# Two attention stages: value products of two heads issued together, projections cut in blocks, rotations moved

## What is computed

```
idx = einsum('bthd,bsd->bths', qi, k_idx)
score = einsum('bth,bths->bts', wi, relu(idx))       # top-k over s picks the keys of the A heads
oa = einsum('bhtk,bkr->bthr', pa, c_sel)             # latent values, then o_a = oa @ w_uv per head
lb = einsum('bthd,bshd->bhts', qb, k_b) + cum_f[t] - cum_f[s]   # causal
ob = einsum('bhts,bshd->bthd', softmax(lb), v_b)
```

```
q, k, v, xq = split(u @ w_in);  q, k = rope(q), rope(k)
p = exp(s - m) / (sum(exp(s - m)) + exp(sink - m));  o = p @ v
```

## Time and profile before

| what | value |
|---|---|
| median of 3 runs | 1451.8 us (1450.42 to 1453.05) |
| profiled execution, its own time | 1447.94 us |
| span of its trace | 1446.6 us, so 1.3 us lie around it |
| PE busy | 1400.8 us, 97% of the span |
| DVE, ACT, POOL busy | 65%, 50%, 16% |
| mean granted PE clock | 0.988 |

### The profile page before, as it was taken

One profiled execution on the slowest core, in us unless ns is written; L12 is line 12 of the kernel. 1 busy time (PEld: TensorE's weight loads), 2 busy tenths in 40 slices (PEclk: granted clock), 3 DMA queues, 4 the chain that ended last, 5 costly groups with the idle time before them and its releaser, 6 DMA issues.

```text
span 1446.6 us, 23175 instructions
## 1 busy us (share of the span) xinstructions
PE 1400.8 (97%) x9623; PEld 1256.9 (87%) x9623; DVE 940.2 (65%) x1510; ACT 723.5 (50%) x1055; POOL 224.3 (16%) x186
## 2 busy tenths in 40 slices
PE   7999999999999999999899999999999999899998
PEld 6887799999898899997777899999689888799997
DVE  4854477667786866667467276566556888666555
ACT  4534355545453555453555464445356775554443
POOL 4561300000000000000722500000123333100000
PEclk9999999999999999999999999999999999899999
DMA  7522145654563456552422355555344435355551
GB/s 279 205 101 117 59 178 201 223 197 178 177 230 140 175 180 227 176 190 102 174 88 88 117 203 176 215 192 177 137 182 147 147 117 205 117 186 200 194 192 58
DMA packets 36698, 240.40 MB, mean 166 GB/s; under 512 B 3889, under 2 KB 6257, under 8 KB 9202
## 3 DMA queue, kind: packets, MB, share of 16 engines
q1 hardware_dynamic: 36594, 238.92, 45.3%
HBM read 236.27 MB, written 2.64 MB: 165 GB/s over the span
## 4 chain that ended last, share of the span: by engine, by line
PE 80%; DVE 9%; ACT 4%; issue 3%; POOL 3%; DMA 2%; SPq 0%; ACTq 0%; DVEq 0%
PE ps L398 22%; PE ps L361 15%; PE ps L362 15%; PE ps L363 15%; POOL wlo L298 2%; ACT whi L290 1%; PE ps L528 1%; DVE ar L2155 1%; PE ps L533 1%; PE ps L855 1%; PE ps L1663 1%; DMA raw<-in_up 1%; DVE wlo L312 1%; PE ps L509 1%; PE ps L1026 1%
## 5 line engine op out<-in xcount | busy, mean ns | idle before, releaser
L361 PE MATMUL ps<-XS,whi 128*128 128x256 f32 x2088 | 599.7, 287 | 4.6 <-DVE wlo L307 2.9
L362 PE MATMUL ps<-XS,whi 128*128 128x256 f32 x2088 | 594.8, 285 | 0.0
L363 PE MATMUL ps<-XS,wlo 128*128 128x256 f32 x2088 | 594.6, 285 | 0.0
L312 DVE TENSOR_TENSOR wlo<-raw,whi 128x2048 fp32r<-128x2048 f32 x163 | 372.4, 2287 | 127.1 <-ACT whi L290 127.1
L290 ACT ACTIVATE whi<-raw 128x2048 fp32r<-128x2048 f32 x203 | 386.9, 1906 | 132.7 <-PE ps L398 81.9
L361 PEld LDWEIGHTS ps<-XS,whi 128*128 128x128 f32 x2088 | 404.8, 194 | 10.8 <-issue 4.5
L362 PEld LDWEIGHTS ps<-XS,whi 128*128 128x128 f32 x2088 | 404.7, 194 | 2.1 <-issue 0.5
L363 PEld LDWEIGHTS ps<-XS,wlo 128*128 128x128 f32 x2088 | 404.5, 194 | 0.0
L398 PE MATMUL ps<-whi,MS 128*128 128x512 f32 x1024 | 290.7, 391 | 0.0
L298 POOL TENSOR_TENSOR wlo<-raw,whi 128x512 fp32r<-128x512 f32 x158 | 207.5, 1346 | 300.2 <-ACT whi L290 216.7
L398 PEld LDWEIGHTS ps<-whi,MS 128*128 128x128 f32 x1024 | 189.8, 188 | 37.5 <-issue 0.4
(11 more groups left out here) (287 smaller groups left out, 1348.7 us busy)
## 6 DMA issues: line engine op xcount, KB each, us to landing
raw<-in_up SPq DMA_DIRECT2D x88, 1024.0 KB, 4.8
raw<-in_down SPq DMA_DIRECT2D x44, 1024.0 KB, 4.8
raw<-in_hg_t SPq DMA_DIRECT2D x16, 1024.0 KB, 4.8
raw<-in_od_t SPq DMA_DIRECT2D x8, 1024.0 KB, 5.4
raw<-in_ev_a SPq DMA_DIRECT2D x6, 1024.0 KB, 9.8
raw<-in_wa_o SPq DMA_DIRECT2D x6, 1024.0 KB, 4.8
raw<-in_hg_o SPq DMA_DIRECT2D x6, 1024.0 KB, 4.9
raw<-in_ev_o SPq DMA_DIRECT2D x4, 1024.0 KB, 6.9
```

What stands on the lines that cost most here:

```text
L312: ve.tensor_tensor(lo[:, 0:w], r[:, 0:w], hi[:, 0:w].bitcast(F32), ALU.subtract).then_inc(w_lo_v)
L361: pe.matmul(d, hi[:, c], S[:, k, 0:256], start=(k == 0), stop=False)
L362: pe.matmul(d, hi[:, c], S[:, k, 256:512], start=False, stop=False)
L363: last = pe.matmul(d, lo[:, c], S[:, k, 0:256], start=False, stop=(k == 7))
```

## The change

`project` can now issue one block at a time. In the even mixer the index scores are issued for two heads in turn (rows 0 to 63, rows 64 to 127), the value products of B heads 2p and 2p+1 together in the odd step, and `post_a` of two heads together in the even step. In the window mixer the value products are issued in pairs as well. Rotation 0 comes behind the projection of the values instead of ahead of it, rotation 1 between the two blocks of `wq+1`, rotations 2 to 4 in steps 1, 3 and 7 instead of 0, 4 and 8. The tiles `wq+2` to `wx+1` go by blocks in steps 0, 1, 5, 6, 8, 9, 11 and 12, where whole tiles stood in steps 3, 7, 10 and 12. ACT's high parts and the DVE's ropes and splits are moved accordingly. The core of the diff:

```diff
-        def project(m, o, ready=None, S=None):
-
-            S = XS if S is None else S
+        def project(m, o, ready=None, blocks=(0, 1)):
+
+            S = XS
-            for i in range(SCHED[m][2] // 1024):
+            for i in blocks[:SCHED[m][2] // 1024]:
...
+            if blocks[-1] == 1:
+                last.then_inc(w_done)
...
-            for h in range(8):
+            for h in range(0, 8, 2):
+
                 pe.wait_ge(e_ac.sem, 3 + h // 4)
                 if h >= 4:
-                    pe.wait_ge(e_re.sem, h - 3)
+                    pe.wait_ge(e_re.sem, h - 2)
                 else:
                     pe.wait_ge(m_ev.sem, 8)
-                q = slice(64 * (h % 2), 64 * (h % 2) + 64)
                 for tt in range(2):
                     a, b = esegs[tt]
                     c = 256 * (h // 2) + 128 * tt
-                    ins = pe.matmul(bank[h % 4][:, a:b], QI[q, c:c + 128], KI[q, 0:b - a], start=True, stop=True)
-                ins.then_inc(e_ix.up())
+                    for r in range(2):
+                        q = slice(64 * r, 64 * r + 64)
+                        ins = pe.matmul(bank[(h + r) % 4][:, a:b], QI[q, c:c + 128], KI[q, 0:b - a], start=True, stop=True)
+                        if tt == 1:
+                            ins.then_inc(e_ix.up())
...
-                if 0 <= i - 4 < 16:
+                if 0 <= i - 4 < 8 and i % 2:
+                    turned_pe(i - 5, 0)
                     turned_pe(i - 4, 0)
-                    value_b(i - 4) if i - 4 < 8 else value_a(i - 12)
-                if 0 <= i - 13 < 8:
-                    post_a(i - 13)
+                    values_b(i - 5)
+                if 8 <= i - 4 < 16:
+                    turned_pe(i - 4, 0)
+                    value_a(i - 12)
+                if 0 <= i - 13 < 8 and i % 2 == 0:
+                    posts_a(i - 14)
...
+        def values_b(h):
+
+            pair_free(h // 2)
             pe.wait_ge(e_ac.sem, AT_VB)
             o = ePAIR[h // 2 % 2]
-            q = slice(64 * (h % 2), 64 * (h % 2) + 64)
-            v = slice(64 * h, 64 * h + 64)
-            pt = ePT[h % 2]
-            pe.matmul(o[q, 0:256], VB[:, v], pt[:, 0:256], start=True, stop=False)
-            pe.matmul(o[q, 128:256], VB[:, 512 + 64 * h:576 + 64 * h], pt[:, 256:384], start=False,
-                      stop=True).then_inc(a_va.up())
+            for r in range(2):
+                pe.matmul(o[64 * r:64 * r + 64, 0:256], VB[:, 64 * (h + r):64 * (h + r) + 64], ePT[r][:, 0:256], start=True, stop=False)
+            for r in range(2):
+                pe.matmul(o[64 * r:64 * r + 64, 128:256], VB[:, 512 + 64 * (h + r):576 + 64 * (h + r)], ePT[r][:, 256:384],
+                          start=False, stop=True).then_inc(a_va.up())
...
+            for r in range(2):
+                pe.wait_ge(e_oa.sem, h + r + 1)
+                pe.matmul(ePAIR[p % 2][64 * r:64 * r + 64, 0:256], WV[:, 64 * (h + r):64 * (h + r) + 64], OA[r], start=True,
+                          stop=True).then_inc(e_po.up())
...
         def window_pe():
             project(wk, bank[4], xs_both(3))
+            accumulate([wv], XS, list(range(8)), 256, [[bank[0]], [bank[1]]], no_wait, True, True)
             filled(3)
             rotate_pe(0, bank[7])
-            accumulate([wv], XS, list(range(8)), 256, [[bank[0]], [bank[1]]], no_wait, True, True)
             project(wq, bank[6])
+            project(wq + 1, bank[5], blocks=(0,))
             pe.wait_ge(r_out.sem, 1)
             rotate_pe(1, bank[7])
+            project(wq + 1, bank[5], blocks=(1,))
...
-                if 0 <= i - 4 < 20:
+                if 0 <= i - 4 < 16 and i % 2:
+                    turned_pe(i - 5, WB)
                     turned_pe(i - 4, WB)
-                    window_value(i - 4) if i - 4 < 16 else cross_value(X0, i - 20, i - 4)
-                for j in range(1, 4):
-                    if i + 2 == 4 * j - 3:
-                        pe.wait_ge(r_in.sem, j + 1)
-                        project(wq + j, bank[6])
-                    if i + 2 == 4 * j - 2:
-                        pe.wait_ge(r_out.sem, j + 1)
-                        rotate_pe(j + 1, bank[7])
-                if i + 2 == 12:
+                    window_values(i - 5)
+                if 16 <= i - 4 < 20:
+                    turned_pe(i - 4, WB)
+                    cross_value(X0, i - 20, i - 4)
+
+                if i in (0, 1):
+                    pe.wait_ge(r_in.sem, 2)
+                    project(wq + 2, bank[6], blocks=(i,))
+                if i in (5, 6):
+                    pe.wait_ge(r_in.sem, 4)
+                    project(wq + 3, bank[6], blocks=(i - 5,))
+                if i in (8, 9):
                     pe.wait_ge(r_in.sem, 5)
-                    project(wx, bank[6])
-                if i + 2 == 14:
+                    project(wx, bank[6], blocks=(i - 8,))
+                if i in (11, 12):
                     pe.wait_ge(r_out.sem, 5)
-                    project(wx + 1, bank[7])
+                    project(wx + 1, bank[7], blocks=(i - 11,))
+                if i in (1, 3, 7):
+                    j = {1: 2, 3: 3, 7: 4}[i]
+                    pe.wait_ge(r_out.sem, j)
+                    rotate_pe(j, bank[7])
...
+        def window_values(i):
+
+            c = i // 2
             o = wV[c % 2]
-            q = slice(64 * r, 64 * r + 64)
-            if r == 0 and c >= 2:
+            if c >= 2:
                 pe.wait_ge(ms_lo.sem, W0 + c - 1)
+            elif c == 1:
+
+                pe.wait_ge(r_in.sem, 3)
             for s in range(2):
-                last = pe.matmul(o[q, 0:256], VN[:, 256 * s + 64 * kvh:256 * s + 64 * kvh + 64],
-                                 wPT[i % 2][:, 256 * s:256 * s + 256], start=(s == 0), stop=(s == 1))
-            last.then_inc(a_va.up())
+                for r in range(2):
+                    kvh = 2 * (c // 4) + r
+                    last = pe.matmul(o[64 * r:64 * r + 64, 0:256], VN[:, 256 * s + 64 * kvh:256 * s + 64 * kvh + 64],
+                                     wPT[r][:, 256 * s:256 * s + 256], start=(s == 0), stop=(s == 1))
+                    if s == 1:
+                        last.then_inc(a_va.up())
...
+            ac.activation(wQ[i % 2], bank[[4, 6, 5, 6, 6][i]][:, :], ACT.Copy, scale=0.125 if i else 1.0).then_inc(r_in.up())
...
             split_act(0)
+            act_weights(wq + 3)
             split_act(1)
+            rope_in_act(2)
+            act_weights(wx)
             for i in range(-2, 26):
-                if i + 2 in (4, 8, 12):
-                    split_act((i + 2) // 4 + 1)
+                if i in (3, 5, 9):
+                    split_act({3: 2, 5: 3, 9: 4}[i])
                 if 0 <= i - 3 < 20:
...
-                for j in range(1, 4):
-                    if i + 2 == 4 * j - 3:
-                        act_weights(wq + j + 2)
-                    if i + 2 == 4 * j - 2:
-                        rope_in_act(j + 1)
-                if i + 2 in (12, 14):
-                    act_weights(wx + (i - 10) // 2 + 2)
-                if i + 2 in (13, 15):
-                    cross_query_act(X0, (i - 11) // 2)
+                if i == 2:
+                    rope_in_act(3)
+                    act_weights(wx + 1)
+                if i == 7:
+                    rope_in_act(4)
+                    act_weights(wo)
+                if i in (10, 13):
+                    j = (i - 10) // 3
+                    cross_query_act(X0, j)
+                    act_weights(wo + 1 + j)
...
-                for j in range(1, 4):
-                    if i + 2 == 4 * j - 1:
-                        rope_dve(j + 1)
-                    if i + 2 == 4 * j:
-                        split_dve(j + 1)
+                if i in (1, 3, 7):
+                    rope_dve({1: 2, 3: 3, 7: 4}[i])
+                if i in (3, 5, 9):
+                    split_dve({3: 2, 5: 3, 9: 4}[i])
```

More of the change, by code:

```diff
@@ L1080, in value_a, with posts_a @@
             pe.matmul(bank[6][:, 128:256], CN[:, 128:256], pt[:, 256:384], start=False, stop=True).then_inc(a_va.up())
-        def post_a(h):
+        def posts_a(h):
             p = 4 + h // 2
-            if h % 2 == 0:
-                pair_free(p)
+            pair_free(p)
             if h == 0:
                 pe.wait_ge(d_wv, 16)
-            pe.wait_ge(e_oa.sem, h + 1)
-            q = slice(64 * (h % 2), 64 * (h % 2) + 64)
-            pe.matmul(ePAIR[p % 2][q, 0:256], WV[:, 64 * h:64 * h + 64], OA[h % 2], start=True, stop=True).then_inc(e_po.up())
+            for r in range(2):
+                pe.wait_ge(e_oa.sem, h + r + 1)
+                pe.matmul(ePAIR[p % 2][64 * r:64 * r + 64, 0:256], WV[:, 64 * (h + r):64 * (h + r) + 64], OA[r], start=True,
+                          stop=True).then_inc(e_po.up())
         def even_act():
```

10 lines of the change are left out of this document (1 added, 9 removed).

## The result

The changed kernel takes 1462.0 us (median of 4 runs, 1459.9 to 1463.4) where before takes 1451.1: 0.75% slower, interval 0.54 to 0.95%. A second comparison (e15) gave 0.46%, interval 0.28 to 0.64%. The prediction was 1449.3 (1444.5 to 1455.5), a gain of 2.5 us. The even mixer did about what was foreseen, and the window mixer lost 12.9 us where the sum had 1.5.

What follows compares the result with a forecast made beforehand. PE was taken to bound the even head loop, with DVE needing nearly as much per window head. Even mixer -4.0 and window mixer +1.5 gave -2.5 us, from 1451.8 to 1449.3, range 1444.5 to 1455.5.

Steps and rivals of the forecast that it cites:

- Column halves: Paired products on PE: matmuls on two column halves run side by side, so a pair costs one member.
- Even mixer, -4.0: Even head loop: value pairs -3.2, posts -1.2, later stall +0.4, sum -4.0 us, bounds 0 and -5.5.
- the posts: Even mixer, heads 0 to 2, in steps that also score: three posts become one pair, 1.16 us less.
- the stall behind it: Even mixer from step 16: the next head's value product waits for DVE's copy behind the post pair, +0.4 us net.
- Window mixer, +1.5: Whole window mixer: reordering -1.5 us plus lower clock +3.0 makes +1.5, bounds -1.5 and +5.
- the DVE chain behind it is as long as before: Window start, rotation 1 to head 0's score: unchanged at 8.1 us, less 0.7 if POOL disturbs less.
- The term for the lower level: Window mixer: lower clock expected twice, 1.7 to 3.4 us each, less the earlier 1.7, so +3.0 us.
- its 1.7: Window mixer: time the kernel before already lost to 6.9 us at the lower clock, subtracted from the new clock cost.
- Window pairs: Window value products in pairs: each saves 1.0 us in steps 5 to 12, the last four only about 0.4 together.
- There PE is the bound: Window steps 5 to 12, with six blocks: PE sets the pace, so each pair saves 1.0 us.
- The tail: Last window heads, no projection left: DVE needs 2.3 us a head; ACT's high parts only trimmed -1.6 to -1.1.
- The slower one: Rival, 21%: window wait for rope 2's split, more lower clock and DVE slowed by POOL; total +1 to +4, about 1454.5.

Runs made afterwards that it cites:

- e15: The changed kernel, unchanged, profiled and compared with before a second time: 1460.5 us, ratio 1.0046.
- e14: The kernel before, unchanged, profiled a second time: 1451.5 us, ratio 0.9995.
- e1: The kernel before with the changed even mixer alone, window mixer as it was: 1444.4 us, ratio 0.9955.
- e4: The changed kernel with ACT's high part of wq+3 behind the split of rope 1 instead of ahead: 1456.1 us, ratio 1.0036.
- e9: The changed kernel with ACT's high part of wx+1 in step 4, behind the exponentials, instead of step 2: 1456.9 us, ratio 1.0028.
- e3: The changed kernel with rotation 0 back ahead of the projection of the values: 1460.7 us, ratio 1.0066.
- e6: The changed kernel with the moves of e3 and e4, and DVE's split of rope 2 ahead of rope 3: 1453.9 us, ratio 1.0007.
- e7: The changed kernel with the low parts of wq, wq+1 and wq+2 written by DVE instead of POOL: 1459.8 us, ratio 1.005.
- e5: The changed kernel with each head's window value product by itself again, unpaired: 1461.1 us, ratio 1.0061.
- e10: The changed kernel with ACT's high parts of steps 10 and 13 behind the exponentials instead of ahead: 1460.2 us, ratio 1.006.
- e11: The changed kernel with the moves of e6, e9 and e10 together: 1451.2 us, ratio 0.9994.
- e13: e11 with rotation 1 ahead of both blocks of wq+1 instead of between them: 1446.5 us, ratio 0.9963.
- e2: e1 plus window value products in pairs at odd steps, nothing else of the window mixer moved: 1446.9 us, ratio 0.9963.
- e12: e1 with a value pair's four matmuls issued head by head instead of alternating column halves: 1446.6 us, ratio 0.9964.

## Why the prediction was right or wrong

**Column halves: right.** A pair of B heads holds PE from 113.52 to 114.32, 0.80 us, where one head held it 0.79.

```profile
113.52 0.65 PE L1051 MATMUL ps<-ar 128*64 128x256 f32 x4
114.00 0.39 PE L1053 MATMUL ps<-ar 128*64 128x128 f32 x4
114.32 0.49 PE L1034 MATMUL ps<-ar 64*128 64x128 f32 x2
```

The rule of the Trainium skill weighed there ("TensorE: Matmul & The Clock Gate", part 3, "The mechanism") would have given 1.6. The rule is on weight loads alone, and that a pair then costs two members was the prediction's reading of it. The trace does not bear it out for column halves.

**Even mixer, -4.0: right in sum, in part by luck.** With equal lower clock (3.4 us each) the head loop is 64.1 us against 66.7 in e14, and with 6.8 us each 65.6 (e15) against 68.3: -2.6 and -2.7. So the loop itself gave 1.3 us less than the 4.0 foreseen. Up to the last score 3.4 us are saved, 3.1 of them value pairs, so the posts gave 0.3 of their 1.2: only two of them stood there, not three. And the stall behind it was sized too small: from the last score on the loop takes 9.8 us instead of 9.0, where the term had +0.4. In exchange PE's wait inside the norm behind it fell from 1.7 to 0.6 us, which no step had; its cause was not looked into. That makes -3.7. The measured -0.45% of e1 (-0.26 to -0.64), about -6.5 us, is compatible with it and does not test it closely. The index scores gave nothing that the profiles tell.

**Window mixer, +1.5: wrong, +12.9.** The step that failed first is "the DVE chain behind it is as long as before". It isn't: ACT's high part of `wq+3` stands in it, and it releases POOL's low parts onto DVE's splits. From rotation 1 to head 0's score it takes 9.9 us, where the sum had 8.1 at most (PE gets to rotation 1 at 711.9 instead of 712.8, since POOL is done with `wv` at 695.6 and not 697.3, and that hides part of it). e4 undoes this and gets 7.3, and a wait of 3.34 us for the 3.6 foreseen. The largest miss lies in the last stretch. The three stretches, with what the prediction's own times give for them:

| stretch | before | foreseen | measured | too small by |
|---|---|---|---|---|
| to head 0's score | 52.5 | 54.4 | 56.5 | 2.1: the wait (6.0 for 3.6) |
| head 0 to head 4 | 15.9 | 17.7 | 22.0 | 4.3: 1.9 wait (4.6 for 2.7), 2.4 clock |
| head 4 to the output | 64.5 | 59.4 | 67.8 | 8.4: 2.4 waits, 6.0 clock |

The first row is e15 against e14, from the window part's start (721.47 - 665.00 and 721.63 - 669.15), since the lower clock ahead of it is alike there. In the second, PE is busy 13.8 us and the prediction's steps add up to 11.4, so 2.4 are put down to the clock. In the last row, PE's work would be 61.8 - 8.1 (pairs) - 1.1 (rotation 3) = 52.6 us and is 58.6, so 6.0 are the clock, and 67.8 - 58.6 = 9.2 are waits where 59.4 - 52.6 = 6.8 were implied. In all 14.8 us, 6.4 of waits and 8.4 of clock. The prediction kept its clock term of +3.0 apart from these times, so 11.8 are left, about the 11.4 between +1.5 and +12.9. Two causes lie under these rows.

- *DVE beside POOL.* The sum took DVE's durations from rows where POOL is mostly quiet. Head 0's division ahead of its transposes was 1.7 us longer for it, and e9 brings the foreseen 2.7 back (2.63). The place of head 4's wait and its size (3.6) were right.
- *The clock.* The term for the lower level ("twice", +3.0) was the right kind and too small. In the changed kernel it falls at 718.5 (6.8 us), 735.5 (13.7), 769.7 (3.4) and 793.6 (3.4), each within 2 us of a wait of 2.4 to 5.9 us or inside one. The last of them comes and goes with its wait: the seven profiles in which head 14's score waits 3.2 us have it within 1.5 us of the end of that wait (both of the changed kernel, e3, e4, e6, e7, e9), and the four in which it waits 1.4 to 1.6 don't (e5, e10, e11, e13). The stretches after head 4's score cost the 6.0 us above, for 5.3 + 3.4 + 3.4 = 12.1 us at 0.5. Gross, 8.4 us where the prediction had 3.0 + 1.7. And its 1.7 were taken off once too often: the prediction's times are laid out at the full clock and are set against starts of before that contain the slow stretch. By its own terms the window mixer should have read -1.5 + 4.7 = +3.2.

**Window pairs: mechanism right, worth wrong.** "There PE is the bound" for steps 5 to 12 failed. Eight pairs save 8.1 us of PE and give 1.4 to 2.0 at most (e5), and nothing by themselves (e2). With DVE at 2.3 us a head so near PE's 2.25, a pair should be a gain only where a block covers DVE. No run tests that.

**The tail.** The prediction saw ACT's high parts in steps 10 and 13 and gave them almost nothing. The second costs a wait of 3.2 us; e10 shows it, and that the waits for DVE's division grow by 2.3 us when 1.8 of it go.

**The rivals.** The slower one had its mechanism and place right (head 4's wait, clock, DVE slowed by POOL) and priced it at +1 to +4. Even and window part together, -3.7 + 12.9, give +9.2, inside the first comparison's interval (+7.8 to +13.8) and at the edge of the second's (+4.1 to +9.3).

**What stays open.** e13's window part is still 1.8 to 3.9 us longer than those with the window mixer of before, with the blocks and ropes 2 to 4 moved. Its run times show no such difference, and it was not taken apart. No run holds the clock and changes the waits or the other way round, so the split between the two is an estimate from busy time. Nor was the gain of the pairs under a block tried.

## What to carry to other kernels

Work that is moved on one engine brings its neighbours' order with it: read each engine's new program between the releaser and the waiting instruction, and count every 2 us instruction that now stands there, before pricing the chain "as before". Price a DVE instruction between SBUF operands by what POOL does beside it. Saving PE time is a gain only where the next engine has slack per item: here 2.3 us of DVE per head ate 8 us of saved matmuls, and the waits of 2.4 us and more were paid again by the lower clock behind them.

## What the hardware showed that was not expected

- A DVE instruction of 0.69 us with SBUF operands alone lasted 8.01 us in the changed kernel, e9 and e10, and 7.98 in e4. It began 0.1 us behind the start of one of POOL's instructions and ended 0.5 us behind the last of POOL's run, six in all. But in e15, the changed kernel again, it also began 0.1 us behind such a start and lasted 1.74. Begun 0.3 to 0.9 us behind one, it lasted 0.96 to 1.49 (before, e3, e6 and the rest), and 0.68 without POOL (e7). So DVE was mostly let in behind POOL's present instruction, and four times only behind POOL's whole run. What decides is not shown. The first instruction of a rope, which reads PSUM, stayed at 0.69 in all of them. The Trainium skill ("SBUF — State Buffer", "SBUF: two separate sides") has such a DVE instruction and GpSimd lock a shared port pair, each for its whole instruction, so that the one that starts second waits. The trace agrees with that in e15, where POOL's next instruction in turn lasted 1.74 us instead of 1.29. A wait through six instructions is more than one lock.
- A small minimum over 128x2 values took up to 1.31 us beside POOL (e4), 0.23 without (e9).
- Matmuls on the two column halves started 0.01 us apart whether their program order alternated or not (e12).
- The lower clock came at the same places of the program for 0 to 10.2 us (435 us) or 3.4 to 10.2 us (103 us), differently from one execution to the next, also where PE had no gap (435 us). Runs of one kernel lie up to 11 us apart (e14: 1445.6 to 1456.3), so 5 us between two single profiles prove nothing.
